# Delta-rule stage: block coefficients and decays spread by transfers through DRAM instead of TensorE, block inverses turned by VectorE, two substitutions interleaved, another order in the last doubling

## What is computed

```
S_t = exp(g_t) S_{t-1} (I - beta_t k_t k_t^T) + beta_t v_t k_t^T,   o_t = S_t q_t
```

## Time and profile before

| | |
|---|---|
| median of 3 runs | 2169.94 us (2169.54 to 2170.11) |
| the profiled execution, its own time | 2169.88 us |
| its span in the profile | 2167.5 us |
| mean granted TensorE clock | 0.999 of full speed |
| DMA | 383.85 MB, mean 177 GB/s |

### The profile page before, as it was taken

The page is one execution under the profiler, slowest core; times in us unless marked ns, Lnnn a source line. Parts: engine busy times, 40 slices in busy tenths (PEclk is TensorE's granted clock), DMA queues, the critical chain, the costliest instruction groups (busy, mean ns, idle before and its releaser), DMA issues.

```text
span 2167.5 us, 35169 instructions
## 1 busy us (share of the span) xinstructions
PE 2155.3 (99%) x12955; PEld 1856.2 (86%) x12955; DVE 1082.4 (50%) x1867; ACT 1045.1 (48%) x1540; POOL 1711.8 (79%) x729
## 2 busy tenths in 40 slices
PE   9999999999999999999999999999999999999998
PEld 8888889888888888888888888888888888888886
DVE  5994243115754163768676745118506704822842
ACT  5444455444557556645455654453333333333343
POOL 7888868877666886657676669888888888888886
PEclk9999999999999999999999999999999999999999
DMA  7666545656454764545465546766666666666664
GB/s 246 187 192 187 183 153 172 191 158 185 137 153 147 234 182 142 153 138 165 138 167 145 156 139 200 213 183 186 189 192 191 186 193 193 189 192 193 190 190 154
DMA packets 321604, 383.85 MB, mean 177 GB/s; under 512 B 14942, under 2 KB 255941, under 8 KB 321221
## 3 DMA queue, kind: packets, MB, share of 16 engines
q1 hardware_dynamic: 317269, 378.06, 58.4%
q10 hardware_dynamic: 4208, 4.00, 0.6%
HBM read 379.92 MB, written 2.10 MB: 176 GB/s over the span
## 4 chain that ended last, share of the span: by engine, by line
PE 96%; DVE 1%; issue 1%; ACT 1%; POOL 0%; DMA 0%; ACTq 0%; SPq 0%; POOLq 0%; DVEq 0%
PE lin_ps L2191 37%; PE lin_ps L2194 18%; PE lin_ps L2217 10%; PE lin_ps L2218 10%; PE lin_ps L2219 10%; PE ps L2154 1%; PE lin_ps L2401 1%; PE lin_ps L2399 1%; PE lin_ps L2400 1%; PE ps L2544 0%; DVE ps L1883 0%; POOL w_lo L635 0%; PE lin_ps L2330 0%; PE lin_ps L2331 0%; PE lin_ps L2329 0%
## 5 line engine op out<-in xcount | busy, mean ns | idle before, releaser
L635 POOL TENSOR_TENSOR w_lo<-raw,w_hi 128x1024 fp32r<-128x1024 f32 (+1 forms) x712 | 1700.7, 2398 | 431.5 <-ACT w_hi L676 324.8
L2191 PE MATMUL lin_ps<-a,w_hi 128*128 128x512 f32 x2176 | 695.5, 401 | 1.2 <-issue 0.5
L676 ACT ACTIVATE w_hi<-raw 128x1024 fp32r<-128x1024 f32 (+1 forms) x452 | 471.1, 1053 | 448.3 <-PE lin_ps L2194 237.0
L2194 PEld LDWEIGHTS lin_ps<-a,w_lo 128*128 128x128 f32 x2176 | 408.7, 188 | 96.3
L2191 PE MATMUL lin_ps<-b,w_hi 128*128 128x512 f32 x1376 | 432.7, 396 | 0.8 <-DVE z L1535 0.8
L2194 PE MATMUL lin_ps<-a,w_lo 128*128 128x256 f32 x2176 | 428.3, 278 | 0.0
L687 ACT ACTIVATE w_hi<-raw 128x1024 fp32r<-128x1024 f32 x228 | 242.1, 1062 | 385.6 <-PE lin_ps L2194 224.2
L2191 PEld LDWEIGHTS lin_ps<-a,w_hi 128*128 128x128 f32 x2176 | 332.6, 189 | 5.5 <-issue 2.6
L2194 PEld LDWEIGHTS lin_ps<-b,w_lo 128*128 128x128 f32 x1376 | 258.5, 188 | 61.0
L2217 PE MATMUL lin_ps<-w_hi,a 128*128 128x512 f32 x752 | 293.3, 390 | 0.0
L2219 PE MATMUL lin_ps<-w_hi,a 128*128 128x512 f32 x752 | 292.7, 389 | 0.0
(11 more groups left out here) (437 smaller groups left out, 2152.2 us busy)
## 6 DMA issues: line engine op xcount, KB each, us to landing
raw<-in_w_in SPq DMA_DIRECT2D x144, 512.0 KB, 3.7
raw<-in_w_mlp_up SPq DMA_DIRECT2D x128, 512.0 KB, 3.8
raw<-in_w_mlp_down SPq DMA_DIRECT2D x128, 512.0 KB, 3.7
raw<-in_even_w_in SPq DMA_DIRECT2D x111, 512.0 KB, 4.4
raw<-in_odd_w_in SPq DMA_DIRECT2D x40, 512.0 KB, 3.7
raw<-in_even_w_out SPq DMA_DIRECT2D x32, 512.0 KB, 4.1
raw<-in_odd_w_out SPq DMA_DIRECT2D x32, 512.0 KB, 4.8
raw<-in_w_o SPq DMA_DIRECT2D x32, 512.0 KB, 4.0
```

Of the source, the lines that this page charges most:

```text
L635: nc.gpsimd.tensor_tensor(w_lo[:, slot, 0:width], raw[:, slot, 0:width], w_hi[:, slot, 0:width].bitcast(F32), ALU.subtract).then_inc(lo_do ...
L676: nc.scalar.activation(w_hi[:, slot, 0:width], raw[:, slot, 0:width], ACT.Copy).then_inc(hi_done, 1)
L2191: nc.tensor.matmul(lin_ps[:, 2 * parity + m, :], hi[:, k, m * P:(m + 1) * P], src[:, kk].rearrange("p s n -> p (s n)"), start=(q == 0 and ...
L2194: last = nc.tensor.matmul(lin_ps[:, 2 * parity + m, 0:T], lo[:, k, m * P:(m + 1) * P], src[:, kk, 0, :], start=False, stop=(q == n - 1 and ...
```

## The change

- The running sums `gc` of the log decays are transposed once for all heads (four small transposes in the Fourier stage), copied by ScalarE and written to a DRAM tensor `gc_far`. For each way a transfer of 128 partitions x 2 KB (`decay_rows`) reads them back, spread over all partitions, at the end of the pair before. `log_sums` is gone; `log_decay` has four instructions of 128 columns and one of 512 where it had two of 512.
- `matrices` leaves its 64 columns as they are. VectorE transposes 32 of them in blocks of 32 x 32. ScalarE issues four transfers (`coefs_out`) to a DRAM tensor `co_far`, in pieces of 64 bytes, then, after a wait for these, one transfer back of 128 partitions x 4 KB (`coefs_in`). `spread` is gone.
- `substitutions` does the 15 steps of both ways alternately, after a wait for the coefficients of both. The coefficients now lie in SBUF, the inverse and the products in PSUM.
- `inverses` expands the inverses and transposes the result on VectorE in blocks of 32 x 32. `turn` and `turned` are gone.
- TensorE's order has `fill(5)` ahead of `grams` and `fill(22)` behind it. Level 6 takes its four matrices in the order 0, 2, 1, 3.

The diff, without the lists of semaphore names and with removed bodies shortened:

```diff
--- before
+++ after
@@ -283,6 +282,12 @@
         out_done = sem("out_done")
+        gc_out = sem("gc_out")
+        gc_in = [sem(f"gc_in{w}") for w in range(2)]
+        co_out = [sem(f"co_out{w}") for w in range(2)]
+        co_in = [sem(f"co_in{w}") for w in range(2)]
+        gc_far = nc.dram_tensor("gc_far", (HN, 4 * P), F32, kind="Internal").ap()
+        co_far = [nc.dram_tensor(f"co_far{w}", (P // BASE, 4 * BASE * BASE), F32, kind="Internal").ap() for w in range(2)]
@@ -424,13 +429,14 @@
                 self.rhs = both
-                self.low_rows, self.top_rows = both[:, 0:4 * HALF * BASE], both[:, 4 * HALF * BASE:6 * HALF * BASE]
+                self.coef = both.rearrange("p (n o q) -> p n o q", n=4, o=BASE)
...
                 self.x = four(two[7])
-                self.inv = own[:, 64 * w:64 * w + 64].rearrange("p (n i) -> p n i", n=4)
-                self.prod = own[:, 128 + 64 * w:192 + 64 * w].rearrange("p (n i) -> p n i", n=4)
+                self.sums, self.inv, self.prod = (self.x_ps[:, 64 * k:64 * k + 64].rearrange("p (n i) -> p n i", n=4) for k in range(3))
+                self.rows = own[:, 64 * w:64 * w + 64].rearrange("p (n i) -> p n i", n=4)
+                self.turned = own[:, 128 + 32 * w:160 + 32 * w]
@@ -1087,6 +1093,11 @@
                     nc.scalar.activation(flat(dsc[:, ER]), flat(dsc[:, REM]), ACT.Exp).then_inc(sc_act.sem, 1)
+                if g == 6:
+                    act.wait_ge(sc_pe.sem, sc_pe.at("rows"))
+                    nc.scalar.activation(scr[0:HN, 3, :], ps[0:HN, 0, :], ACT.Copy).then_inc(sc_act.sem, 1)
+                    act.wait_ge(sc_act.sem, sc_act.at("rows"))
+                    act.dma_start(gc_far, scr[0:HN, 3, :]).then_inc(gc_out, 16)
@@ -1135,14 +1146,30 @@
+                def decay_rows(w, k):
+
+                    act.dma_start(w.x.rearrange("p a n -> p (a n)"),
+                                  gc_far[2 * k + w.w:2 * k + w.w + 1, :].broadcast_to([P, 4 * P])).then_inc(gc_in[w.w], 16)
+
+                def coefs_out(w):
+
+                    from_dve(w, "dl")
+                    far = co_far[w.w].rearrange("b (n o q) -> b n o q", n=4, o=BASE)
+                    for n in (2, 3):
+                        act.dma_start(far[:, n], w.rows[:, n, :]).then_inc(co_out[w.w], 16)
+                    from_dve(w, "tp")
+                    far = co_far[w.w].rearrange("(g e) (h r q) -> g e h r q", e=2, h=2, q=BASE)
+                    for e in range(2):
+                        act.dma_start(far[:, e, 0], w.turned[:, e * BASE:(e + 1) * BASE]).then_inc(co_out[w.w], 16)
+
+                def coefs_in(w):
+                    act.wait_ge(co_out[w.w], 64 * (p + 1))
+                    act.dma_start(w.coef.rearrange("p n o q -> p (n o q)"),
+                                  co_far[w.w].unsqueeze(1).broadcast_to([P // BASE, BASE, 4 * BASE * BASE])).then_inc(co_in[w.w], 16)
...
-
-                def turned(w):
-                    from_pe(w, "tr3")
-                    halves_ = w.rhs.rearrange("p (a n) -> p a n", a=4)
-                    nc.scalar.activation(halves_[:, 0:4:3, :], w.y_ps.rearrange("p (a n) -> p a n", a=2), ACT.Copy).then_inc(dn_act[w.w].sem, 1)
@@ -1178,6 +1205,9 @@
                     act.wait_ge(bld, 4)
+                    act.wait_ge(gc_out, 16)
+                    for w in ways:
+                        decay_rows(w, 0)
@@ -1197,8 +1227,13 @@
                 keep_m(one_way)
-                fill(13, 14)
+                coefs_out(one_way)
+                fill(13)
                 keep_m(other)
+                coefs_in(one_way)
+                coefs_out(other)
+                fill(14)
+                coefs_in(other)
@@ -1206,9 +1241,7 @@
                         nc.scalar.activation(gate, gate, ACT.Sigmoid).then_inc(mx_act.sem, 1)
-                turned(one_way)
                 fill(21)
-                turned(other)
@@ -1221,6 +1254,9 @@
                     out_norms(w)
+                if p < PAIRS - 1:
+                    for w in ways:
+                        decay_rows(w, p + 1)
@@ -1781,9 +1817,6 @@
             dve.wait_ge(mk, done("c"))
-            nc.vector.tensor_tensor(same, in_block[:, 0], in_block[:, 1], ALU.add).then_inc(mk, 1)
-            dve.wait_ge(mk, done("s"))
-            nc.vector.tensor_tensor(same, same, ident[:], ALU.add).then_inc(mk, 1)
@@ -1892,10 +1925,12 @@
                     own, y = dn_dve[w.w].sem, four1(w.y_ps)
-                    from_pe(w, "gc")
-                    nc.vector.tensor_tensor(y, y, per(GC, w), ALU.subtract).then_inc(own, 1)
-                    after(w, "dsub")
-                    nc.vector.scalar_tensor_tensor(out=y, in0=y, scalar=0.0, in1=dmask[:], op0=ALU.min, op1=ALU.add).then_inc(own, 1)
+                    dve.wait_ge(gc_in[w.w], 16 * (p + 1))
+                    from_act(w, "vt")
+                    for n in range(4):
+                        nc.vector.tensor_scalar(y[:, n, :], w.x[:, n, :], col(GC, n // 2, n % 2, w), 0.0, ALU.subtract, ALU.min).then_inc(own, 1)
+                    after(w, "dsub3")
+                    nc.vector.tensor_tensor(y, y, dmask[:], ALU.add).then_inc(own, 1)
@@ -1911,40 +1946,38 @@
                     after(w, "blk")
...
+                    nc.vector.tensor_reduce(w.sums, w.x.rearrange("p n (b i) -> p n i b", i=BASE), AX.X, ALU.add).then_inc(own, 1)
                     after(w, "red")
...
+                    nc.vector.tensor_tensor(w.rows, w.sums, nth.unsqueeze(1).broadcast_to([P, 4, BASE]), ALU.add).then_inc(own, 1)
                     after(w, "dl")
...
-                def substitution(w):
...
+                    nc.vector.transpose(w.turned, w.rows[:, 0:2, :].rearrange("p n i -> p (n i)")).then_inc(own, 1)
+                    nc.vector.tensor_reduce(w.inv, nth.unsqueeze(1).broadcast_to([P, 4, BASE]).unsqueeze(3), AX.X, ALU.add).then_inc(own, 1)
+
+                def substitutions():
+
+                    for w in ways:
+                        dve.wait_ge(co_in[w.w], 16 * (p + 1))
+                    for n in range(1, BASE):
+                        for w in ways:
+                            after(w, f"su{n - 1}" if n > 1 else "one")
+                            nc.vector.tensor_tensor(w.prod[:, :, 0:n + 1], w.coef[:, :, n, 0:n + 1], w.inv[:, :, 0:n + 1],
+                                                    ALU.mult).then_inc(dn_dve[w.w].sem, 1)
+                        for w in ways:
+                            after(w, f"pr{n}")
+                            nc.vector.tensor_reduce(w.inv[:, :, n:n + 1], w.prod[:, :, 0:n + 1], AX.X, ALU.add).then_inc(dn_dve[w.w].sem, 1)
+
+                def inverses(w):
                     own = dn_dve[w.w].sem
...
                     after(w, f"su{BASE - 1}")
...
                         nc.vector.tensor_tensor(w.tu[:, at:at + 2, :].rearrange("p c (b i) -> p c b i", i=BASE),
...
+                                                w.inv[:, 2 * d:2 * d + 2, :].unsqueeze(2).broadcast_to(wide),
                                                 which.unsqueeze(2).unsqueeze(1).broadcast_to(wide), ALU.mult).then_inc(own, 1)
+                    for d, at, to in ((0, 4, 0), (1, 2, 6)):
+                        after(w, f"ex{d}")
+                        nc.vector.transpose(w.tu[:, to:to + 2, :].rearrange("p c n -> p (c n)"),
+                                            w.tu[:, at:at + 2, :].rearrange("p c n -> p (c n)")).then_inc(own, 1)
@@ -2036,8 +2067,9 @@
                 group_out(7 * p + 2)
+                substitutions()
                 for w in ways:
-                    substitution(w)
+                    inverses(w)
@@ -2638,6 +2670,11 @@
                     m.then_inc(sc_pe.sem, 1)
+                if g == 5:
+                    pe.wait_ge(sc_dve.sem, sc_dve.at("rem"))
+                    for n in range(4):
+                        m = nc.tensor.transpose(ps[0:HN, 0, n * P:(n + 1) * P], dsc[:, GC, n // 2, n % 2, :], ident[:])
+                    m.then_inc(sc_pe.sem, 1)
@@ -2660,14 +2697,6 @@
                         m = nc.tensor.transpose(blk(w.y_ps, c), blk(w.v_feat, c), ident[:])
...
-                def log_sums(w):
...
-                        m = nc.tensor.matmul(blk(w.y_ps, n), dsc[:, GG, n // 2, n % 2, h:h + 1].broadcast_to([P, P]), tri[:, n // 2, :],
...
@@ -2679,18 +2708,6 @@
-                def spread(w):
...
-                    nc.tensor.matmul(w.x_ps, same, w.low_rows, start=True, stop=True).then_inc(dn_pe[w.w].sem, 1)
...
-                    nc.tensor.matmul(w.y_ps[:, 0:4 * HALF * HALF], same, w.top_rows, start=True, stop=True).then_inc(dn_pe[w.w].sem, 1)
...
-                def turn(w):
...
-                        m = nc.tensor.transpose(blk(w.y_ps, n), w.tu[:, at, :], ident[:])
...
@@ -2699,13 +2716,14 @@
+                def turns(l):
+
+                    return (0, 2, 1, 3) if l == 6 else range(4)
...
                     for w in ways:
-                        if l == 4:
-                            from_act(w, "tt")
-                        else:
```

(59 more changed lines are left out.)

17 lines of the change are left out of this document (4 added, 13 removed).

## The result

The changed kernel took 2181.19 us (median of 5 runs, 2178.96 to 2183.04) against 2170.11 for the kernel before (5 runs, 2169.54 to 2170.45): ratio 1.0051, 95% interval 1.0039 to 1.0064. It is slower by 11 us, where 2148.3 was predicted, in a range up to 2157. The profiled execution took 2182.86 us, its span 2181.1.

A forecast was written before the change was run, and what follows sets the result against it. TensorE was taken to bound the kernel: 20.9 us saved over four pairs, plus 1.1 for level 6, less 0.4 for added transposes, makes 21.6; 2169.88 - 21.6 = 2148.3 us, own range 2146.5 to 2149.5, whole range 2146.5 to 2157.

The forecast's parts named there:

- the forecast one: Period of one pair, TensorE busy without a gap: 93.2 to 93.5 us.
- 5.23: TensorE's work removed per pair, in us: log_sums 1.78, spread 2.58, turn 0.87.
- level 6: TensorE's new matrix order alternates array corners: saves between nothing and 2.2 us in all, 1.1 taken.
- 21.6: Total fall of TensorE's work in us: 20.9 + 1.1 - 0.4.
- 60 instructions: VectorE's substitutions of both ways, interleaved: 7.5 us taken; 13.7 us without overlap.
- a way's inverses: VectorE's expansions and transposes after the substitutions: 4 x 0.35, 1.4 us for a way.
- The rival without overlap: VectorE's substitutions stay at 13.7 us, inverses 4.6 us late ahead of level 4: 2166.7 us, chance 0.07.
- a small transfer lands after 2.9: Coefficient writes from ScalarE's queue: landing priced at 2.9 us, from rows of 2.8 to 4.1 us.
- the read of 512 KB, 5.0: Coefficients' read back ahead of the substitutions: lands after 5.0 us, low end 3.7, high end 6.4.
- The cover: Slack before TensorE wants weight unit 15, fed by ScalarE's rounding 15 and GpSimd: 1.4 us.
- The rival that ends slower: Scattered coefficient writes land after 6.4 us, rounding 15 starts 7 us late, GpSimd and TensorE starve: 2175 us, chance 0.06.
- the point of decision: Slow scattered writes decide the outcome once a pair's wait exceeds 5.4 us.

The follow-up runs named there:

- one row for all: Changed kernel with the other way's writes issued ahead of the first read, each way's read taking one weight row for all 128 partitions: 2154.37 us, ratio 0.9928.
- Writes first: Changed kernel with the second way's writes issued ahead of the first way's read: 2164.46 us, ratio 0.9981; repeats took 2169.0 and 2165.96 us.
- the one-level kernels: Second way's writes ahead of the first read, reads from 128 adjacent weight rows or from one row: 2156.10 and 2154.37 us.
- the half read: Changed kernel reading only the forward direction's coefficients, 256 KB per way: 2161.43 us in its own order, 2154.25 us with second way's writes ahead of first read.

## Why the prediction was wrong

The forecast and its misses, on the changed kernel's profiled execution: 2148.3, plus 21.8 us of waits in the four pairs (20.4 for GpSimd, 1.4 issue), plus 10.0 of half clock, is 2180.1, against 2182.86. The half clock is counted where TensorE works: the four pairs have four stretches at clock 0.50, 23.9 us long, with 20.09 us of matmuls in them (their windows summed), and half of that is lost.

```profile
sum 23.91, PE 20.09 PEld 17.13 DVE 9.55 ACT 10.56 POOL 22.43; mean PE 5.02 PEld 4.28 DVE 2.39 ACT 2.64 POOL 5.61
```

The same sum for one row for all: 2148.3 + 3.2 + 1.7 = 2153.2, against 2154.2.

In the order of the prediction's steps, with G the end of the Gram matrices (1003.9 there; 1008.71 + 1.79 = 1010.5 in the changed kernel, from its timeline):

| step | predicted | measured |
|---|---|---|
| first way's writes issued | G + 6.2 | G + 6.9 |
| first read issued | G + 9.1 | G + 10.4 |
| other way's writes issued | G + 11.3 | G + 13.5 |
| second read issued | G + 14.2 | G + 20.3 |
| coefficients there | G + 19.2 | G + 27.6 |
| other way's inverses ready | G + 29.5 | G + 37.4 |

Where nothing is late, the period is the forecast one. The kernel with one row for all has such a pair, from its Gram matrices to the next pair's (window: length, then TensorE's busy us):

```profile
1096.01:1189.36 93.35, 93.35 (x859) 82.34 (x858) 63.38 (x201) 50.98 (x98) 66.58 (x29) 1.00 0.59 176
```

- **Right in the main: TensorE bounds the kernel, and its work falls nearly as summed.** A pair of one row for all without any wait lasts 93.35 us (the line above): 5.39 under the 98.74 before, for 5.23 and level 6. Level 6 gave less than taken: the second eight still start 0.28 behind the first (1062.14 - 1061.86), as in the earlier trace rows, and last 0.40 for 0.45, so that what follows starts 0.05 sooner in each of its two steps, 0.4 us in all for 1.1. In the changed kernel TensorE's busy time fell by 8.2 us with 10.0 of half clock in it, so the work by 18.2, for 21.6. Of the 3.4 us between, 0.7 are level 6; about 2 lie in the pairs with waits, which come to 93.8 to 94.1 us without idle time and half clock. Why, no run shows.
- **Right: VectorE.** 7.07 us for 60 instructions, 0.118 each, for 7.5; 1.35 for a way's inverses, for 1.4. The rival without overlap is out, and the Trainium skill's rule ("VectorE: DVE Perf Modes", The DRAIN you can't avoid), that the next instruction does not start until the pipe is empty, did not bind two chains that take turns: in the pair shown the next one started 0.08 to 0.14 us behind one that lasts 0.16 to 0.23. The section itself says that an instruction which is not held starts earlier, which the prediction left out.
- **The step that failed: "a small transfer lands after 2.9", used for the second way's writes.** The first way's took 3.4, which is near it. The second way's took 6.9. The row that I priced it from is of a transfer with nothing ahead of it; here 512 KB stood ahead in the same queue. The prediction listed the queue of ScalarE's instructions and not the queue of its transfers. The semaphore's record shows the order: the read's last update came at 1029.0, the first of these writes' data 0.1 to 0.2 us later, and their last at 1030.8. Writes first took this away (6.9 to 3.4) and 16.7 us with it. The 6.1 us between G + 14.2 and G + 20.3 are these 4.0, 0.5 for the first way's landing (3.4 for 2.9), 0.7 up to the end of its issues (four took 2.38 us where 1.8 were taken) and 0.9 for the five issues that follow (3.12 us, 0.62 each, for 0.45 as in the earlier trace rows).
- **The second failed step: "the read of 512 KB, 5.0".** It took 7.3 in the pair shown (6.5 to 8.2 over the pairs), and 6.4 to 10.2 with writes first. The value would have been right for a source of one level (3.7 to 5.1, once 6.7); the broadcast of 1 MB in the earlier trace rows was of that kind, and the coefficients' read is not. In the changed kernel it cost nothing at level 4, since TensorE was late already; with writes first it is most of what is left, and the one-level kernels, at 2154 and 2156, show its price: 11.4 and 12.9 us, each beside a two-level kernel on its own chip.
- **The cover was right, and the rival's place too.** The prediction gave rounding 15 a cover of 1.4 us and said that past it GpSimd and TensorE starve. Rounding 15 started at G + 21.1, not at G + 14.6, 6.5 late; less 1.4 that is 5.1, and TensorE was idle for 5.0. The rival that ends slower had the place and the point of decision (a wait of over 5.4 in a pair), but the wrong mechanism: it wanted slow scattered writes, for which the Trainium skill ("DMA: Bandwidth & Descriptors", Specifications) speaks with its rule on pieces under 512 bytes. The first way's writes, in pieces of 64 bytes, landed after 3.4 us, so they were not slow here, and bigger pieces did not help.
- **The unpriced term: the clock.** 5.0 us of wait is less than 5.4, and by waits alone the kernel would have stayed near the time before: 2148.3 + 21.8 = 2170.1. The half clock, 10.0 us in sum, is most of what made it slower; 2.8 us are the work that did not fall. The prediction priced a wait at its own length.

## What to carry to other kernels

When a transfer is put on a queue, ask what stands ahead of it in bytes as well as in instructions: a small write behind a big read lands after the read, and a wait for it in an in-order engine holds everything behind. Take a transfer's price from a row with the same form of source, not only of the same size; how many updates its semaphore gets in a trace tells over how many engines it was dealt. And price a gap of TensorE that is several us long with the clock behind it: here 5.0 us of idle time cost 8.0.

## What the runs showed of the hardware that was not expected

- A read of 512 KB whose source has two levels (8 by 16 rows of 4 KB) took 6.4 to 11.0 us beside the weights' stream, with eight updates of its semaphore as data landed; the same bytes from a source of one level took 3.7 to 5.1 (once 6.7) with 16, whether from 128 rows or one.
- In the changed kernel four small writes landed 3.4 to 3.5 us after the last issue, and 6.6 to 6.9 us when a read of 512 KB was ahead of them in the queue; 3.3 to 3.8 with 256 KB ahead.
- After 4.3 us without work TensorE had clock 0.50 for 5.9 us of full work. In the other three pairs gaps of 4.1 to 4.3 us were followed by 3.2 to 5.7 us of it. A gap of 1.7 us was followed by 3.4 us of it in one row for all, one of 1.9 us by none in the half read.
- Two VectorE chains of dependent small instructions, taking turns, ran at 0.118 us for an instruction; one alone at 0.228.
- VectorE transposed 128 x 256 in blocks of 32 x 32 in 0.42 us (median of the changed kernel), two in a row in 0.76.
